# A decoder layer on one core: attention divided by its sums late, heads in pairs on half the array, and three small products in column tiles

## The reference

```python
q, k, v, qi, ki, wi, p, ga, gb = project(rms_norm(x, g_mix), w_in)
dots  = jnp.einsum('bqhd,bld->bqhl', qi, ki_all)             # indexer: 8 heads, one key of 64
score = jnp.einsum('bqh,bqhl->bql', wi, jax.nn.relu(dots))   # causal, then top 128 (prompt) or 256 (sample) keys
logits = q @ kg * 64 ** -0.5 + rel_bias[t5_bucket(dist)]
p = softmax(logits);  attn = p @ vg
merged = sigmoid(ga) * (attn @ w_br_attn) + sigmoid(gb) * (pooled_mix @ w_br_pool)
x = x + merged @ w_out
x = x + moe_ffn(rms_norm(x, g_ffn))     # top 4 of 32 clamped-SwiGLU experts
y = rms_norm(x, g_final)
```

## Time and profile before

| | |
|---|---|
| three runs | 1843.65, 1855.12, 1860.61 us, median 1855.12 |
| the profiled execution's own time | 1848.48 us |
| its span, first to last instruction | 1846.6 us |
| PE / PE weight load / DVE / ACT / POOL busy | 95% / 44% / 29% / 17% / 12% |
| mean granted TensorE clock | 0.962 of 2.4 GHz |
| projections and indexer, up to 252 us | (a) to (d) |
| prompt attention | 423 to 510 us |
| output projection and router | 544 to 627 us |
| experts | 650 to about 1790 us |

### The profile page before, as it was taken

The page is one execution under the profiler, slowest core; times in us unless marked ns, Lnnn a source line. Parts: engine busy times, 40 slices in busy tenths (PEclk is TensorE's granted clock), DMA queues, the critical chain, the costliest instruction groups (busy, mean ns, idle before and its releaser), DMA issues. The chain is left out here.

```text
span 1846.6 us, 34280 instructions
## 1 busy us (share of the span) xinstructions
PE 1750.8 (95%) x14367; PEld 821.1 (44%) x14367; DVE 539.2 (29%) x1011; ACT 308.1 (17%) x622; POOL 214.3 (12%) x276
## 2 busy tenths in 40 slices
PE   6999999998899699999999999999999999999996
PEld 5667657775474333333333333333333333333332
DVE  3227927806722411121112111211211211221123
ACT  2221011004401111111111111111111111111112
POOL 4600510004400000000000000000000000000000
PEclk9899999998899799999999999999999999999996
DMA  6323764722063369999999999999999999999963
GB/s 217 118 94 111 256 208 131 243 83 103 1 237 124 130 256 342 360 350 391 378 336 372 388 336 362 382 385 381 375 386 350 357 391 383 377 379 384 338 258 105
DMA packets 71168, 515.13 MB, mean 279 GB/s; under 512 B 10322, under 2 KB 11154, under 8 KB 45890
## 3 DMA queue, kind: packets, MB, share of 16 engines
q1 hardware_dynamic: 60826, 485.91, 67.2%
q0 software_dynamic: 10288, 28.52, 7.0%
HBM read 491.64 MB, written 22.96 MB: 279 GB/s over the span
## 5 line engine op out<-in xcount | busy, mean ns | idle before, releaser
L1131 PE MATMUL PS<-weight_ring,region_experts 128*32 128x512 f32 x6144 | 677.4, 593 | 0.0
L1131 PEld LDWEIGHTS PS<-weight_ring,region_experts 128*32 128x32 f32 x6144 | 189.8, 110 | 434.3 <-issue 422.7
L824 PE MATMUL PS<-region_x,region_w 128*128 128x268 f32 x1152 | 268.1, 393 | 0.3 <-ACT region_x L719 0.3
L1137 PE MATMUL PS<-weight_ring,act_turned 128*32 128x512 f32 x2048 | 242.7, 616 | 2.1
L824 PEld LDWEIGHTS PS<-region_x,region_w 128*128 128x128 f32 x1152 | 219.7, 192 | 45.0 <-issue 3.4
L1427 DVE TENSOR_SCALAR region_experts<-PS 128x512 f32<-128x512 f32 x32 | 22.1, 692 | 537.4 <-PE PS L1131 537.4
L609 POOL DMA_INDIRECT y_acc<-region_x,idx_i x32 | 46.2, 1445 | 767.1 <-issue 767.1
L1137 PEld LDWEIGHTS PS<-weight_ring,act_turned 128*32 128x32 f32 x2048 | 65.0, 113 | 137.3 <-issue 124.8
L1143 PE MATMUL PS<-weight_ring,act_turned 128*32 128x256 f32 x2048 | 123.0, 380 | 0.0
L774 ACT ACTIVATE act_turned<-PS 128x384 f32<-128x384 f32 x32 | 15.7, 490 | 470.0 <-PE PS L1169 470.0
L1143 PEld LDWEIGHTS PS<-weight_ring,act_turned 128*32 128x32 f32 x2048 | 63.3, 110 | 57.5 <-issue 24.5
(11 more groups left out here) (246 smaller groups left out, 1393.1 us busy)
## 6 DMA issues: line engine op xcount, KB each, us to landing
weight_ring<-w_gu SPq DMA_DIRECT2D x128, 2048.0 KB, 9.5
weight_ring<-w_down SPq DMA_DIRECT2D x64, 2048.0 KB, 10.6
region_w<-w_mt SPq DMA_DIRECT2D x33, 512.0 KB, 4.0
weight_ring<-cache_kT SPq DMA_DIRECT2D x64, 256.0 KB, 3.9
weight_ring<-cache_v SPq DMA_DIRECT2D x64, 256.0 KB, 3.9
weight_ring<-w_out SPq DMA_DIRECT2D x2, 2048.0 KB, 9.7
weight_ring<-bias_strip SPq DMA_DIRECT2D x1, 2560.0 KB, 12.8
region_x<-xT SPq DMA_DIRECT2D x4, 536.0 KB, 5.3
```

The lines of the kernel that those rows point to most:

```text
L824: mm = pe.matmul(PB[j % 2][0:rows, a, 0:HALF], lhs(k), rhs(k)[:, HALF * a:HALF * a + HALF], start=(k == 0), stop=(k == nk - 1))
L1131: mm = pe.matmul(out[GRP * j:GRP * j + GRP], hTe[:, k, GRP * g:GRP * g + GRP], weights(c)[:, k, :], start=False, stop=(k == KD - 1))
L1137: pe.matmul(bank(3)[GRP * j:GRP * j + GRP], actT[:, k, GRP * g:GRP * g + GRP], w_dn[:, k, 512 * q:512 * q + 512], start=(k == 0), stop=(k ...
```

## The change

- (b) and the key tile: the key's 64 columns stand once in the weights, followed by the 8 head weights and zeros. ACT copies 8 rows of the result to `wiT`, then the key rows twice to `kiT`. PE makes the per-row weights by 5 transposes of `wiT`. The load `w_wi` is gone.
- (c): one buffer `qiT`, no zeros. Even heads use partitions 0 to 63 of both operands, odd heads 64 to 127. Four PSUM buffers `DB` (two of them the projections' `PB`), so the k projections now wait for the last relu.
- Sample indexer: `zi` has 32 columns per sample pair; four column tiles take the place of four accumulated products. `relu_s` and `wblk` have 128 partitions. POOL writes `wcol` with four DMAs where it had one.
- (f): `normalise` is gone. `turn` waits for the exponential. The order of tiles is 4, 0, 1, 2, 3. PE issues logits(2m), logits(2m+1), turn(2m-2), turn(2m-1), values. Heads use the 64 partitions of their own in `qT` and `kT`; the copy and memset that made zeroed queries are gone. Per row tile DVE spreads the reciprocals of 8 sums over 64 columns each (`spread_sums`), PE transposes that into PSUM bank 1 (`turn_sums`), and DVE multiplies the tile's output in place (`scale_out`).
- v, last 24 rows: four column tiles of 128 columns. Output projection, last 24 rows: four column tiles of 256 columns, and four smaller adds.

The diff, cut to its core:

```diff
-        qi_v = [part(QI, 0, 4, NT), part(W6, 0, 4, NT)]
+        qiT = part(QI, 0, 4, NT)
+        DB = [AB[0], AB[1], PSF[:, 0:1024], PSF[:, 1024:2048]]
+        RX = bank(1)
-        HEADS = [(t, h) for t in range(NTILE) for h in range(H)]
+        ORDER = (4, 0, 1, 2, 3)
+        HEADS = [(t, h) for t in ORDER for h in range(H)]
...
-            take(J_KI, halves(kiT), wide(J_KI)).then_inc(S["act_taken"], 1)
+            take(J_KI, halves(wiT[0:H]), wide(J_KI)[64:64 + H]).then_inc(S["wiT_in"], 1)
+            act.activation(halves(kiT[0:64]), wide(J_KI)[0:64], ACT.Copy)
+            act.activation(halves(kiT[64:P]), wide(J_KI)[0:64], ACT.Copy).then_inc(S["act_taken"], 1)
...
-            pe.wait_ge(S["small_in"], 96)
+            pe.wait_ge(S["wiT_in"], 1)
             for t in range(NTILE):
-                for k in range(KD):
-                    mm = pe.matmul(PB[J_WI % 2][0:TROWS[t], 0, H * t:H * t + H], hT[:, k, P * t:P * t + TROWS[t]], wi_sb[:, k, :], ...)
+                mm = pe.transpose(PB[J_WI % 2][0:TROWS[t], 0, H * t:H * t + H], wiT[0:H, P * t:P * t + TROWS[t]], ident[0:H, 0:H])
...
-                if i >= 2:
-                    pe.wait_ge(S["relu_done"], i - 1)
+                if i >= 4:
+                    pe.wait_ge(S["relu_done"], i - 3)
+                hp = 64 * (h % 2)
-                    mm = pe.matmul(AB[i % 2][0:ROWS[t], a:z], qi_v[h % 2][:, h // 2, P * t:P * t + ROWS[t]], kiT[:, a:z], ...)
+                    mm = pe.matmul(DB[i % 4][0:ROWS[t], a:z], qiT[hp:hp + 64, h // 2, P * t:P * t + ROWS[t]], kiT[hp:hp + 64, a:z], ...)
+            pe.wait_ge(S["relu_done"], len(DOTS))
             for c in range(4):
                 project(J_K + c, w, hk, KD)
-            pe.wait_ge(S["relu_done"], len(DOTS))
...
-                    mm = pe.matmul(PSF[0:64, 4 * 512 + lo:4 * 512 + hi], zi[:, 64 * j:64 * j + 64], kidx[:, j, lo:hi], start=(j == 0), stop=(j == 3))
+                    mm = pe.matmul(PSF[32 * j:32 * j + 32, 4 * 512 + lo:4 * 512 + hi], zi[:, j, :], kidx[:, j, lo:hi], start=True, stop=True)
...
-                pe.wait_ge(S["p_norm"], i + 1)
+                pe.wait_ge(S["exp_done"], i + 1)
...
+            def turn_sums(n):
+                r = ROWS[ORDER[n]]
+                pe.wait_ge(S["rsum_set"], n + 1)
+                pe.wait_ge(S["ao_scaled"], n + 1)
+                for c in range(4):
+                    mm = pe.transpose(RX[:, c * r:c * r + r], rsum_x[0:r, 2 * c:2 * c + 2, :].rearrange("p a d -> p (a d)"), ident[0:r, 0:r])
+                mm.then_inc(S["rsumT_ready"], 1)
+            for m in range(1, PAIRS + 2):
+                if m < PAIRS:
+                    logits(2 * m)
+                    logits(2 * m + 1)
+                if m <= PAIRS:
+                    turn(2 * m - 2)
+                    turn(2 * m - 1)
+                if m >= 2:
+                    values((2 * m - 4) % H // 2, (2 * m - 4) // H)
+                if m % 4 == 1 and m > 4:
+                    turn_sums(m // 4 - 1)
...
+                    for k in range(KD):
+                        for q in range(4):
+                            mm = pe.matmul(PB[j % 2][32 * q:32 * q + r, 0, 0:256], sga[:, k, P * t:NT], wo[q // 2][:, k, 256 * (q % 2):256 * (q % 2) + 256], ...)
...
-                dve.tensor_scalar(p, p, rsum[0:ROWS[t], i:i + 1], None, ALU.mult).then_inc(S["p_norm"], 1)
+            def spread_sums(n):
+                L(dve.reciprocal(rsum[0:r, H * n:H * n + H], esum[0:r, H * n:H * n + H]))
+                dve.tensor_copy(rsum_x[0:r], rsum[0:r, H * n:H * n + H].unsqueeze(2).broadcast_to([r, H, HD])).then_inc(S["rsum_set"], 1)
+            def scale_out(n):
+                dve.wait_ge(S["ao_taken"], n + 1)
+                dve.wait_ge(S["rsumT_ready"], n + 1)
+                dve.tensor_tensor(o, RX[:, 0:4 * r].rearrange("p (c r) -> p c r", c=4), o, ALU.mult).then_inc(S["ao_scaled"], 1)
...
+                if i > H and h == 1:
+                    spread_sums(i // H - 1)
+                if i > H and h == 7:
+                    scale_out(i // H - 1)
```

More of the change, by code:

```diff
@@ L169, in build_step @@
         mix_sb = part(W6, slot(2) + 3312, PG, P)
-        wi_sb = part(W6, slot(2) + 3824, KD, H)
+        wiT = part(W6, slot(0), NT)
         vexp = part(W6, slot(2) + 2208, 2, AW)
@@ L196, in build_step @@
         btmp = KI[:, :]
-        qz = [qi_v[0], qT]
+        rsum_x = part(W6, slot(5) + 2640, H, HD)
         wo = [part(W6, slot(n), KD, 512) for n in range(2)]
@@ L480, in _ @@
             link(po, po.memset(zi, 0.0), "po_step", n)
-            po.wait_ge(S["small_in"], 96)
+            link(po, po.memset(wcol, 0.0), "po_step", n)
+            po.wait_ge(S["small_in"], 80)
             for b in range(NS):
@@ L568, in _ @@
                     po.wait_ge(S["attn_s_done"], 2)
-                if h == 0 and t:
-                    po.wait_ge(S["mask_done"], t)
+                if i == 0:
+                    po.wait_ge(S["mask_done"], 4)
                 if i >= 2:
@@ L643, in _ @@
             for c in range(4):
[L644 to L645 removed]
+                take(J_QI + c, halves(qiT[:, c, :]), wide(J_QI + c)).then_inc(S["act_taken"], 1)
             act.wait_ge(S["h_done"], KD)
[L647 removed]
+            take(J_KI, halves(wiT[0:H]), wide(J_KI)[64:64 + H]).then_inc(S["wiT_in"], 1)
+            act.activation(halves(kiT[0:64]), wide(J_KI)[0:64], ACT.Copy)
+            act.activation(halves(kiT[64:P]), wide(J_KI)[0:64], ACT.Copy).then_inc(S["act_taken"], 1)
             act.wait_ge(S["proj_done"], J_WI + 1)
@@ L728, in _ @@
                     pt_out(i - 2)
-                if h == 3 and t:
-                    ao_out(t - 1)
+                if h == 3 and i > H:
+                    ao_out(i // H - 1)
             pt_out(len(HEADS) - 2)
@@ L1021, in turn, with values @@
                 mm.then_inc(S["pt_ready"], 1)
-            def values(c, t):
-                i = H * t + 2 * c
+            def values(c, n):
+                i = H * n + 2 * c
+                t = ORDER[n]
                 r = ROWS[t]
                 pe.wait_ge(S["pt_taken"], i + 2)
-                if c == 0 and t >= 2:
-                    pe.wait_ge(S["ao_taken"], t - 1)
+                if c == 0 and n >= 2:
+                    pe.wait_ge(S["ao_taken"], n - 1)
                 for a in range(0, KEYS[t], P):
@@ L1037, in _ @@
             pe.wait_ge(S["act_taken"], J_A)
-            pe.wait_ge(S["qz_done"], 1)
-            pe.wait_ge(S["qz_zero"], 1)
             logits(0)
             pe.wait_ge(S["attn_s_done"], 2)
-            for i in range(1, len(HEADS) + 3):
-                if i < len(HEADS):
-                    logits(i)
-                if 2 <= i < len(HEADS) + 2:
-                    turn(i - 2)
-                if i >= 4 and i % 2 == 0:
-                    values((i - 4) % H // 2, (i - 4) // H)
-            pe.wait_ge(S["ao_taken"], NTILE)
+            logits(1)
+            def turn_sums(n):
[5 more added lines that the diff above has]
+                mm.then_inc(S["rsumT_ready"], 1)
+            PAIRS = len(HEADS) // 2
+            for m in range(1, PAIRS + 2):
[9 more added lines that the diff above has]
+                    turn_sums(m // 4 - 1)
+            pe.wait_ge(S["ao_scaled"], NTILE + 1)
             pe.wait_ge(S["lgp_done"], len(HEADS))
@@ L1214, in _ @@
             dve.memset(pool_b[:, 0:PAD], 0.0).then_inc(S["pool_pad"], 1)
-            for hp in range(2):
-                dve.memset(qi_v[hp][64 - 64 * hp:128 - 64 * hp], 0.0).then_inc(S["qi_zero"], 1)
             dve.wait_ge(S["bgu_in"], 16)
@@ L1349, in _ @@
                 dve.wait_ge(S["proj_done"], j + 1)
-                x1 = xn(t)[0:r].rearrange("p (a b) -> p a b", a=2)
-                dve.tensor_tensor(x1, PB[j % 2][0:r], x1, ALU.add).then_inc(S["dve_taken"], 1)
+                if t < 4:
+                    x1 = xn(t).rearrange("p (a b) -> p a b", a=2)
+                    dve.tensor_tensor(x1, PB[j % 2], x1, ALU.add).then_inc(S["dve_taken"], 1)
+                else:
+                    for q in range(3):
+                        x1 = xn(t)[0:r, 256 * q:256 * q + 256]
+                        dve.tensor_tensor(x1, PB[j % 2][32 * q:32 * q + r, 0, 0:256], x1, ALU.add)
+                    x1 = xn(t)[0:r, 768:D]
+                    dve.tensor_tensor(x1, PB[j % 2][96:96 + r, 0, 0:256], x1, ALU.add).then_inc(S["dve_taken"], 1)
                 if t == 0:
@@ L1521 @@
     gates = np.stack([tiles(gb), tiles(ga)], axis=1).reshape(2 * KD, P, KD, P)
-    w_mt = np.concatenate([tiles(qi), tiles(np.concatenate([ki, ki], axis=1)), tiles(k), tiles(q), tiles(p), gates])
+    w_mt = np.concatenate([tiles(qi), tiles(np.concatenate([ki, wi, np.zeros((D, P - HD - H), np.float32)], axis=1)), tiles(k), tiles(q), tiles(p), gates])
     def rows4(w):
```

126 lines of the change are left out of this document (64 added, 62 removed).

## The result

| | before | changed |
|---|---|---|
| median | 1849.38 us (1836.03 to 1860.61, 4 runs) | 1800.71 us (1782.05 to 1804.06, 4 runs) |
| profiled execution, its span | 1848.48, 1846.6 us | 1799.6, 1797.9 us |
| first product of the experts (a bias product) starts | 649.69 us | 597.90 us |
| last bias product of gate and up starts | 1791.05 us | 1742.32 us |

The ratio is 0.974, 95% interval 0.9686 to 0.9794. A second timing of the same changed kernel gave 0.9738 (0.970 to 0.9775). The prediction was 1800 us, with 1780 to 1822 as its range. Ratios leave out executions that took over 1.5% more than the fastest of the same kernel.

A forecast was written before the change was run, and what follows sets the result against it. PE, busy 95% of the span, was taken to bound the kernel. Terms 11.0 + 5.3 + 3.8 + 22.8 + 1.5 + 9.8 = 54.2 us, all ahead of the experts, gave 1800 us, range 1780 to 1822.

The forecast's parts named there:

- Head weights and key tile: Ahead of the indexer: first indexer product at 67.2 us where it was 75.71, a gain of 8.5 us.
- Indexer products: The 32 prompt indexer products: head halves overlap, DVE's chain sets the pace; 11.0 us together with the key tile, bounds 8 and 13.
- v tail: Last 24 rows of v: 64 column-tiled records at 0.05 us each, 3.2 us for 7.03; 3.8 us saved, bounds 3.3 and 5.2.
- Attention: Prompt attention: 87.0 us falls to 64.2 without the per-head normalisation and with overlapping halves; 22.8 us, bounds 12 and 31.
- logits 0.97 once if the halves overlap: Attention, PE's time per pair with 512 keys: both heads' logits cost 0.97 us once, in a sum of 3.35 us.
- first rival: Indexer and attention: products on array halves don't overlap, so two logits cost two; gain 36 us, time 1819 us, chance 0.14.
- tile 4's last two pairs and one more us in tile 1: Attention, allowance for half clock: tile 4 has two pairs at 3.0 and two at 4.6 us; tile 1 takes 8.8 + 1.
- The sign named as disproof: Attention: a granted clock below 0.8 would show the forecast wrong, as would a pair's logits standing one behind the other.
- second rival: Attention: halves overlap, but thin work holds the clock at half all through; 3 us lost there, time 1831 us, chance 0.07.
- Output projection's tail: Last 24 rows of the output projection: 13.91 us falls to 3.8, 0.3 added for adds; 9.8 us, bounds 5 and 10.5.
- Slower: Indexer and attention: half-array products neither overlap nor keep the clock; 18 us slower, 1873 us, chance 0.02.
- Given back in the experts: Experts: transfers, not PE, might set the pace and take back the cut work; if half goes 1828 us, chance 0.04.

The follow-up runs named there:

- padded_dots: The changed kernel with indexer products on zero-padded 128 rows as before, four PSUM buffers kept; one time 1771.35 us.
- norm_back: The changed kernel with DVE normalising each head again before its transposes, pairs and half arrays kept; attention 94.9 us, one time 1807.69 us.
- padded_logits: The changed kernel with attention logits on all 128 array rows, zeros in the queries' other half; attention 61.8 us, one time 1798.29 us.
- single_heads: The changed kernel with attention heads issued one at a time, late division and half arrays kept; attention 110.5 us, one time 1845.25 us.

## Why the prediction was right, and where it was not

**Time and sign** came out: 1800 for 1800.71 us, 54.2 us forecast ahead of the experts and 51.8 found. That the time came out to 1 us is luck, as the last paragraph of this section shows.

**Head weights and key tile**: 8.5 us, as worked out; the first product starts at 67.23 for 67.2, and at 65.9 to 68.0 in the twelve executions with this edit, so the second digit is chance. **Indexer products**: 25.0 us for 24.3. DVE's chain is the pace in the wide tiles, and its price right. The 1.1 us charged for the clock were 2.1. The bound for halves that don't overlap (8) overstated their weight: `padded_dots` has no halves and is 1.2 us faster. "Before, PE set the pace" held for the 16-row tile alone. What remains is the later start of DVE's chain before, 2.66 us behind the first product for 1.8 now, and the four buffers; no run separates them.

**Sample indexer** 5.5 for 5.3, **v tail** 4.6 for 3.8: 5.1 in its own records, 0.5 given back behind them. The mis-sized term is the record of 24 rows by 128 columns: 0.05 us assumed, 1.9 us for 64 found, 0.03 each. ACT's four copies, costed at nothing, are 0.24 us of that, as a wait.

**Attention**: 21.1 for 22.8, and the mechanism named first was right: the waits for L1310 are gone, and `norm_back` shows 21.7 us of them when the line returns. Two steps failed though, in opposite directions. The step "logits 0.97 once if the halves overlap" counted the overlap as a gain; the bound for no overlap charged 13 us for it, and `padded_logits`, which has none, is 1.5 to 4.1 us faster. (The bound was also added up wrongly: 22.8 less 13 is 9.8, not 12. The first rival would then be at 1821, still inside the range.) Only at full clock do halves gain (3.2 us in tiles 2 and 3). And the step that let tile 4's last two pairs and one more us in tile 1 be slow was too short: the clock stood at 0.50 for 33 us, to the end of tile 1. The total held by luck: tile 4 was 2.1 us cheaper and tile 2 1.3 cheaper than priced, against 2.2, 2.3 and 0.7 too little in tiles 0, 1 and 3.

The sign named as disproof, a clock below 0.8, did occur. That was a badly chosen sign. The second rival (halves overlap, half clock all through, 0.07) had the right mechanism for the first half of the stretch, and I had read PE's busy share as what would keep the clock up. Before the change the clock was full with PE busy for 12.01 of 16 us (tile 2) and 15.28 of 20 (tile 3). The Trainium skill, "TensorE: Matmul & The Clock Gate", section "What's actually happening", says too that the clock follows how busy PE has been; here PE shows 33.00 of 33.00 us busy at 0.50, so the profile's busy column is no measure of that.

**Branch product** 2.8 for 1.5: it runs at full clock throughout, where I had taken half of the loss as staying. **Output projection's tail** 8.5 for 9.8 (7.7 to 9.7 by the spread of this stage): the product itself fell from 13.91 to 3.65 us as said, but tile 3's norm is no longer hidden, and PE waits 1.58 us for its copy. The prediction named that chain as the reason for its low bound and didn't cost it in the term.

**First rival** (halves don't overlap, 0.14): false, 1.06 us for four records. Its price was wrong as well. **Slower**: a pair neither side by side nor at full clock is what `single_heads` built, 110.5 us, 23.5 more than before and even with late division, close to the 25 us more that this rival gave the attention. So its chance of 0.02 stood on the overlap alone. **Given back in the experts**: -3.1 us in this pair of traces, well inside the 42 us over which that stretch ranges. **Whole time**: ahead of the experts my sum was 2.4 us too large, in the experts 3.1 were lost, and the median of the changed kernel lay 1.1 us above its profiled execution where I had taken 6.6. So 5.5 us too little and 5.5 too much cancel.

## What to carry to other kernels

Move a per-row scale behind the product it scales, where the chain between two engines' turns is what PE waits for: with tile 4 first, that was worth 13.5 of 87 us. Use half of the array for pairs only where the pair is what sets the time and PE's clock is full; in a thin stretch zero padding to all 128 rows was faster by 1.5 to 4.1 us, and dearer by only 0.8 us of PE per pair of 512 keys. Column tiles for few-row outputs brought what they promised, 19.1 us for three small products.

## What the runs showed of the hardware that I had not expected

- With products on 64 rows one at a time the clock stayed down, 0.51 over 95 us with PE busy 93.43 (`single_heads`); with padded operands in the same order it was 0.93.
- The same DVE multiplication of 384 elements took 1.25 or 1.52 us with the width of POOL's addition beside it (384 or 512), which took 1.00 or 1.27. One of 512 took 1.59 us beside an addition and 0.48 without.
- Column-tiled products of 24 rows by 128 columns went at 0.03 us a record, those of 256 columns at 3.65 / 64 = 0.057 us.
- Waits for gathered rows are 30.7 us of a spread of 41.6 between kernels whose experts' code is the same.
